# Interleaved weight halves and reversed dense passes in a two-block transformer kernel on one core

## The reference

```
h  = rms(x) * g1                # 512 x 1024
z  = h @ w_in                   # RWKV, retention, window attention, and 3 gates of 1024
x += (sum of sigmoid(gate_b) * (mixer_b(z) @ w_o_b)) @ w_out
x += (silu(rms(x)*g2 @ w_gate) * (rms(x)*g2 @ w_up)) @ w_down
```

## Time and profile before

| quantity | us |
|---|---|
| median of 2 runs | 2548.85 (2546.43 to 2551.27) |
| the profiled execution | 2548.05 |
| span of its instructions | 2546.2 |
| PE busy | 2511.3, 99% of the span |
| POOL busy | 1512.5, 59% |
| DVE busy | 1311.4, 52% |

### The profile page before, as it was taken

One profiled execution on the slowest core, in us unless ns is written; L12 is line 12 of the kernel. 1 busy time (PEld: TensorE's weight loads), 2 busy tenths in 40 slices (PEclk: granted clock), 3 DMA queues, 4 the chain that ended last, 5 costly groups with the idle time before them and its releaser, 6 DMA issues.

```text
span 2546.2 us, 47105 instructions
## 1 busy us (share of the span) xinstructions
PE 2511.3 (99%) x16344; PEld 2012.3 (79%) x16344; DVE 1311.4 (52%) x1979; ACT 691.6 (27%) x1290; POOL 1512.5 (59%) x963
## 2 busy tenths in 40 slices
PE   8989999999999999999999999999999999999999
PEld 6868888887877778888888888867678888888887
DVE  7867555465566657663322224566647663322224
ACT  4452000024135446521100002134446531100002
POOL 5666666656646455556666666645454556666665
PEclk9999999999999999999999999999999999999999
DMA  4213222223211122223222223211122223222223
GB/s 167 71 43 119 91 99 99 91 86 117 92 51 52 44 97 69 72 87 103 93 97 99 96 93 122 91 47 50 51 97 67 75 87 103 91 99 95 95 99 99
DMA packets 72442, 222.55 MB, mean 87 GB/s; under 512 B 9312, under 2 KB 12256, under 8 KB 72288
## 3 DMA queue, kind: packets, MB, share of 16 engines
q1 hardware_dynamic: 71856, 220.36, 26.3%
q10 hardware_dynamic: 432, 0.14, 0.0%
HBM read 218.37 MB, written 2.10 MB: 87 GB/s over the span
## 4 chain that ended last, share of the span: by engine, by line
PE 92%; DVE 4%; DVEq 1%; issue 1%; DMA 1%; POOL 1%; ACT 0%; ACTq 0%; POOLq 0%; SPq 0%
PE acc L550 80%; PE bank L550 10%; DMA raw<-in_w_pg 1%; PE bank L1214 0%; POOL w_lo L376 0%; DVE sumsq L1252 0%; DVE y_lo L1252 0%; DVE bank L1252 0%; DVE xg_lo L1345 0%; POOL w_hi L369 0%; DVE bank L1611 0%; DMA vec<-in_vec 0%; DVE att L1464 0%; DVEq L1412 0%; DVEq L1709 0%
## 5 line engine op out<-in xcount | busy, mean ns | idle before, releaser
L376 POOL TENSOR_TENSOR w_lo<-raw,w_hi 128x1024 fp32r<-128x1024 f32 (+3 forms) x438 | 961.8, 2196 | 301.3 <-PE acc L550 242.1
L369 POOL TENSOR_SCALAR w_hi<-raw 128x1024 fp32r<-128x1024 f32 (+3 forms) x438 | 438.2, 1000 | 584.1 <-PE acc L550 503.1
L550 PE MATMUL acc<-xg_hi,w_hi 128*128 128x512 f32 x2208 | 581.8, 397 | 6.7 <-DVE xg_lo L1345 2.9
L550 PE MATMUL acc<-xg_lo,w_hi 128*128 128x512 f32 x2208 | 568.8, 393 | 0.0
L550 PE MATMUL acc<-xg_hi,w_lo 128*128 128x512 f32 x2208 | 562.7, 393 | 0.2 <-POOL w_lo L376 0.2
L550 PEld LDWEIGHTS acc<-xg_hi,w_hi 128*128 128x128 f32 x2208 | 408.6, 188 | 107.1 <-issue 20.9
L550 PEld LDWEIGHTS acc<-xg_hi,w_lo 128*128 128x128 f32 x2208 | 411.3, 188 | 88.4 <-issue 1.5
L550 PEld LDWEIGHTS acc<-xg_lo,w_hi 128*128 128x128 f32 x2208 | 411.2, 188 | 87.4 <-issue 1.5
L2131 ACT ACTIVATE ffn_act<-ffn_t 128x512 f32<-128x512 f32 x100 | 63.2, 632 | 742.6 <-DVEq L1312 600.7
L1252 DVE TENSOR_TENSOR x<-x,acc 128x512 f32<-128x512 f32 x104 | 71.3, 686 | 311.1 <-PE acc L550 310.6
L1252 DVE TENSOR_TENSOR bank<-acc,rstd 128x512 f32<-128x512 f32 x72 | 50.3, 699 | 263.4 <-PE acc L550 263.3
(11 more groups left out here) (351 smaller groups left out, 2708.4 us busy)
## 6 DMA issues: line engine op xcount, KB each, us to landing
raw<-in_w_up SPq DMA_DIRECT2D x132, 512.0 KB, 3.2
raw<-in_w_down SPq DMA_DIRECT2D x48, 512.0 KB, 3.2
raw<-in_w_gate SPq DMA_DIRECT2D x48, 512.0 KB, 3.2
raw<-in_w_ret SPq DMA_DIRECT2D x32, 512.0 KB, 3.3
raw<-in_w_rw SPq DMA_DIRECT2D x28, 512.0 KB, 3.2
raw<-in_w_o SPq DMA_DIRECT2D x48, 256.0 KB, 2.7
raw<-in_w_in SPq DMA_DIRECT2D x18, 512.0 KB, 3.2
raw<-in_w_down SPq DMA_DIRECT2D x24, 384.0 KB, 3.0
```

The costliest lines, as they stand in the source:

```text
L369: nc.gpsimd.tensor_scalar(w_hi[:, s, 0:n], raw[:, s, 0:n], 1.0, 0.0, ALU.mult, ALU.add).then_inc(w_half[s], 1)
L376: nc.gpsimd.tensor_tensor(w_lo[:, s, 0:n], raw[:, s, 0:n], bits(w_hi[:, s, 0:n]), ALU.subtract).then_inc(w_split[s], 1)
L550: return nc.tensor.matmul(o, a, b, start=first, stop=last, skip_group_check=shared)
```

## The change

It does three things.

1. `w_hi` and `w_lo` become one tensor `halves` of shape (2, 1024, 2): a column's high half and its low half are neighbours, and `w_hi`, `w_lo` are views of it with a step of 8 bytes between columns. The tile that PE loads is spread over 1024 bytes instead of 512. POOL's two instructions write, and one of them reads, with that step. Every tile begins at remainder 128 modulo 512 (high) or 132 (low).
2. A new helper `dense` reverses the token order of a pass: the activations are read from the last token to the first, and PSUM is written in that order. Every dense pass goes through it. The other matmuls stay as they are.
3. The split activations get start remainders of their own: xg 256, y (first block) 192, z_rw, z_rt and with them y1, y2, hid 320, emb 256. The distance from the weight tiles, which was 0, becomes 128 bytes for xg and emb, 64 for y of the first block, 192 for y1, y2 and hid. The assertion that all are equal goes.

```diff
-LINE, START = 512, 128
+LINE = 512
...
-        xg_hi, _ = place("xg_hi", (DC, T), F32R, line=START)
-        xg_lo, _ = place("xg_lo", (DC, T), F32R, line=START)
+        xg_hi, _ = place("xg_hi", (DC, T), F32R, line=256)
+        xg_lo, _ = place("xg_lo", (DC, T), F32R, line=256)
...
-        raw, _ = place("raw", (2, DC * P), line=START)
-        w_hi, _ = place("w_hi", (2, DC * P), F32R)
-        w_lo, _ = place("w_lo", (2, DC * P), F32R)
+        raw, _ = place("raw", (2, DC * P), line=128)
+        halves, _ = place("halves", (2, DC * P, 2), F32R)
+        w_hi, w_lo = (halves[:, :, :, h] for h in range(2))
...
-        y_hi, _ = place("y_hi", (DC, T), F32R, line=START)
-        y_lo, _ = place("y_lo", (DC, T), F32R, line=START)
+        y_hi, _ = place("y_hi", (DC, T), F32R, line=192)
+        y_lo, _ = place("y_lo", (DC, T), F32R, line=192)
...
-        z_rw, rw_at = place("z_rw", (14, T), line=START)
+        z_rw, rw_at = place("z_rw", (14, T), line=320)
...
-        emb_at = base + 24 * 1024 + (START - base) % LINE
+        emb_at = base + 24 * 1024 + (256 - base) % LINE
...
+            def dense(o, a, b, first, last, shared=False):
+
+                return mm(o[:, ::-1], a, b[:, ::-1], first, last, shared)
...
-                        last = mm(o[:], columns_of(w, s, k), v[:, c, :], v is hi and m == 0 and k == 0, m == 1 and k == n - 1)
+                        last = dense(o[:], columns_of(w, s, k), v[:, c, :], v is hi and m == 0 and k == 0, m == 1 and k == n - 1)
...
```

More of the change, by code:

```diff
@@ L180, in build @@
         emb, _ = place("emb", (2, T), F32, offset=emb_at + C4)
-        assert {a % LINE for a in (rw_at, rt_at, emb_at)} == {START} and emb_at + 3 * C4 // 2 <= rt_at and base + 4 * sum(int(np.prod(shape)) for _, shape in FIRST) <= emb_at
+        assert emb_at + 3 * C4 // 2 <= rt_at and base + 4 * sum(int(np.prod(shape)) for _, shape in FIRST) <= emb_at
         rw = {}
@@ L592, in late @@
                     for k, c in enumerate(chunks[:-1]):
-                        mm(acc[s][:], columns_of(w_lo, s, k), a[0][:, c, :], False, False)
+                        dense(acc[s][:], columns_of(w_lo, s, k), a[0][:, c, :], False, False)
                     if stat is not None:
@@ L606, in late @@
                     pe.sem_inc(pe_turn, 1)
-                    mm(acc[s][:], columns_of(w_hi, s, k), a[0][:, c, :], i == 0, False)
-                    last_hi = mm(acc[s][:], columns_of(w_hi, s, k), a[1][:, c, :], False, False)
-                    last = mm(acc[s][:], columns_of(w_lo, s, k), a[0][:, c, :], False, i == n - 1)
+                    dense(acc[s][:], columns_of(w_hi, s, k), a[0][:, c, :], i == 0, False)
+                    last_hi = dense(acc[s][:], columns_of(w_hi, s, k), a[1][:, c, :], False, False)
+                    last = dense(acc[s][:], columns_of(w_lo, s, k), a[0][:, c, :], False, i == n - 1)
                 last_hi.then_inc(hi_done[s], 1)
@@ L620, in three @@
             def three(s, a, k, first, last):
-                mm(acc[s][:], columns_of(w_hi, s, k), a[0][:, k, :], first, False)
-                hi_pass = mm(acc[s][:], columns_of(w_hi, s, k), a[1][:, k, :], False, False)
-                return hi_pass, mm(acc[s][:], columns_of(w_lo, s, k), a[0][:, k, :], False, last)
+                dense(acc[s][:], columns_of(w_hi, s, k), a[0][:, k, :], first, False)
+                hi_pass = dense(acc[s][:], columns_of(w_hi, s, k), a[1][:, k, :], False, False)
+                return hi_pass, dense(acc[s][:], columns_of(w_lo, s, k), a[0][:, k, :], False, last)
             def hid_slots(I, n, count, ahead=0):
@@ L817, in _ @@
                 w = columns_of(w_hi, 0, c)
-                mm(acc[0][:], w, xg_hi[:, c, :], c == 0, False)
-                last = mm(acc[0][:], w, xg_lo[:, c, :], False, False)
+                dense(acc[0][:], w, xg_hi[:, c, :], c == 0, False)
+                last = dense(acc[0][:], w, xg_lo[:, c, :], False, False)
             last.then_inc(hi_done[0], 1)
@@ L822, in _ @@
             for c in full:
-                last = mm(acc[0][:], columns_of(w_lo, 0, c), xg_hi[:, c, :], False, c == DC - 1)
+                last = dense(acc[0][:], columns_of(w_lo, 0, c), xg_hi[:, c, :], False, c == DC - 1)
                 if c < DC - 1:
@@ L833, in one @@
                 def one(s, w, v, c, first=False, last=False):
-                    return mm(acc[s][:], columns_of(w, s, c), v[:, c, :], first, last, True)
+                    return dense(acc[s][:], columns_of(w, s, c), v[:, c, :], first, last, True)
                 def started(s):
@@ L888, in part @@
                         w, v, c = (w_hi, w_hi, w_lo)[k // DC], (xg_hi, xg_lo, xg_hi)[k // DC], k % DC
-                        last = mm(acc[s][:], columns_of(w, s, c), v[:, c, :], k == 0, k == 3 * DC - 1, True)
+                        last = dense(acc[s][:], columns_of(w, s, c), v[:, c, :], k == 0, k == 3 * DC - 1, True)
                         if k == 2 * DC - 1:
```

10 lines of the change are left out of this document (5 added, 5 removed).

## The result

The changed kernel takes 2603.31 us (median of 2 runs, 2602.49 to 2604.13) against 2548.85: the ratio is 1.0219, with an interval of 1.0201 to 1.0238. It is slower by 54 us, where 96 us less were forecast. Its profiled execution took 2604.13 us with a span of 2602.3.

The account below looks back on a forecast made before the run. The prediction took PE's dense passes to bound the kernel. From 2548.05 us, minus 98 (pace), minus 5 (first passes), plus 8 (less hidden) gave 2453; likeliest case 2440 to 2475, wide range 2440 to 2600.

Parts of the forecast that it names:

- What bounds the kernel: Opening step: PE busy 99% at full clock; dense passes set the time, each 226.7 ns, 13.3 beyond its columns.
- Part 1: Pace of the dense passes: reversed order, 8-byte columns and distances keep weight and activation reads apart, 98 us less.
- the price of 216.3 ns: Assumed length of a dense pass after the change, 213.3 + 3 ns, taken from the float32 overhead.
- The 5 us for first passes: Further gain: some 240 stretches begin out of phase, about 4 passes each 5 ns over the pace.
- The sign named for them: Sign of being right: first passes behind small matmuls run at the same pace as later ones.
- no gain: Rival for the dense passes: the 10.4 ns stay, pace 226.7, time 2535 to 2560; chance 0.20.
- Slower, by a denser weight read: Rival: a tile over 1024 bytes doubles the 10.4 ns, a pass 237 ns, 2646 or 2673 us; chance 0.17.
- partial: Rival: only xg passes gain, or all gain half; 2483 or about 2500, between 2475 and 2525; chance 0.16.
- the term of minus 98 us: Main term of the sum: 9408 dense passes, each 10.4 ns shorter.
- Part 2: POOL's split instructions with 8-byte step: no change taken; covered by PE until they grow by a factor of 1.5.
- Part 3: What becomes late: shorter passes hide less DVE and ACT work in RWKV pairs and at stage starts; 8 us back.
- its 8 us: Loss added to the sum: half of 8 us gained in RWKV pairs, and as much again at stage starts.

Follow-up runs that it names:

- e5: Kernel before with 19 series of 48 dense-like passes appended on PE, one thing varied per series: 226.7 ns a pass as before, 233.3 with activations backwards.
- e6: Kernel before with 35 other series of 48 passes appended, varying repeated tokens, shifts, tile width and pass length: 215.8 ns with 8 tokens repeated, 241.9 with 16.
- e1: Kernel before with only the token order of the dense passes reversed, halves contiguous, all start remainders 128: 2599.07 us, ratio 1.020.
- e2: Kernel before with only the weight halves interleaved (8-byte columns), passes forward, all starts at 128: 2601.69 us, ratio 1.0211.
- e3: Kernel before with only the activations' start remainders changed, halves contiguous, passes forward: 2592.71 us, ratio 1.0177.
- e4: Changed kernel without its new distances: 8-byte columns and reversed order, all start remainders 128: 2614.28 us, ratio 1.0263.
- e8: Kernel before with the weight halves moved 16 bytes later (low halves 16 + 256), passes forward: 2584.97 us, ratio 1.0145.
- e9: Kernel before with dense passes taking tokens in runs of 32 bytes at every 128 bytes, PSUM written alike: 2567.11 us, ratio 1.0074.

## Why the prediction was wrong

**What bounds the kernel** was right: PE at 99% with a full clock, and the passes' pace sets the time. So was the arithmetic of the lever: a shift of 6.67 ns a pass is 58 us.

**Part 1 failed** at the step "some 10.4 ns appear only where the moving operand streams at full rate ... two read streams that meet in the same part of SBUF could", and with it at the price of 216.3 ns. The first half holds: float32 passes have 429.2 = 426.7 + 2.5 ns, repeated tokens 215.8 = 213.3 + 2.5, and at 1.2 GHz passes of the plain kind have 426.7 and no surcharge at all (e5). The second half doesn't. Loads of 32 columns or of one repeated column leave 231.8 and 231.7 (e5), and a backward read keeps its 20 ns beside a load of 32 columns (e6). The surcharge doesn't shrink with what the load reads; a quarter of the columns to load makes the pass longer by 5 ns. What a pass without any load would take, no run shows. That the pace depends on phase was read rightly; the 230 ns of first passes were passes ahead of a good state, 226.7, into which distance 0 always settled. Nothing in the trace of before showed a pass of 512 columns without a full load beside it, so the share of the load was an inference; one short series could have measured it.

From this the three edits fall one by one. Reversal: it costs 6.67 ns by itself (e1; in the series 233.3 with PSUM forward, 226.7 with only PSUM backwards). 8-byte columns: the same (e2), with no gain from the matched pace; all six distances give 233.3. Distances: they lose the good state (e3: 232.5 and 233.3), and in the changed kernel the two other edits have lost it already; there they only keep the passes out of the 236.7 ns of e4.

The 5 us for first passes didn't come either. The sign named for them did, first and later passes at the same pace (233.5 and 233.3 ns by starts), but because the later ones became as slow as the first.

The Trainium skill's rule of two independent read ports (TensorE: Matmul & The Clock Gate, Part 2) was put under "no gain". The runs agree with it in that a smaller load doesn't shorten the pass; that the place of the load still moves the pace by 2 to 7 ns is more than it says. The 215.7 ns that the Trainium skill gives there for 512 columns were met here only with at most 8 tokens repeated, or with each of 256 taken twice (215.8).

**The rivals.** "Slower, by a denser weight read" had the sign and, with 2646, was 43 us too high; its mechanism fell, since e1 reads as dense as before and costs the same. What its sentence on PSUM left open is measured in e5: PSUM written in reversed order has 226.7 ns, no cost. "No gain" and "partial" fell. The range ended at 2600 and the result is 2603.3: the prediction weighed a price for PSUM written backwards and none for activations read backwards, though the trace before has no row of such a read. In the sum, the term of minus 98 us (10.4 ns a pass) should have been plus 58 (6.67 ns a pass, less the first passes).

**Part 2** was right: POOL's instructions grew by 8% and 1%, far from the 1.5 at which they would have mattered, and PE waited 1.0 us for them (0.7 + 0.3).

**Part 3** was right that nothing becomes late, with 3.4 us against 3.3; its 8 us were for shorter passes, which didn't come.

**What stays open.** Why a forward read has a good state of 13.3 ns and others 18 to 20, why the step lies between 32 and 64 bytes, whether the period is 256 bytes for every distance, what sets the cycle into which a stretch falls, and whether the surcharge would be there without any load. The runs show these figures and not the structure behind them.

## What to carry to other kernels

Before a stall is put down to two streams that meet, run the pass with one of them made tiny: 48 passes with a 32-column tile would have taken away the reason for this change, and 48 read backwards would have priced it. Change order, step and distance one at a time: three edits with one common condition each cost the whole, and their sum says nothing. And a pace from a bare series is one of the states of that pass; only the kernel, with its interruptions, tells which it gets (220.0 in a series; in the kernel 220.0 and 230.7, in the mean 228.8). Look at the pace stretch by stretch: the mean of 234 in e4 hid two paces, 233.3 and 236.7.

## What the runs showed of the hardware

- A float32r pass of 512 columns at 2.4 GHz costs 213.3 + 2.5 ns when its activations cover at most 32 bytes or each is taken twice; with 64 bytes repeated it takes 241.9, with 128 bytes 236.6, and from 256 bytes on 226.7 (e6). At the granted 1.2 GHz it takes 426.7, which is its columns alone (e5).
- Activations read backwards cost 20 ns a pass over the columns, forwards 13.3 at distance 0; PSUM written backwards costs nothing (e5).
- The distance between the weight tile's and the activations' start counts and not their addresses: 226.7 at 0 and 256 bytes, 228.9 at 64 and 320, 232.2 to 233.5 at most others. A full 128-column load at distance 0 makes the pass 5 ns shorter than a 32-column load does (e5, e6).
- Paces are repeating cycles of intervals, and a stretch keeps its cycle for hundreds of passes. The same pass, order and distance can fall into different ones within one execution: 226.7 and 233.3 in e8, 220.0 and 230.7 in e9, 233.3 and 236.7 in e4. At distance 0, forwards, with contiguous columns, all 18 long stretches had 226.7.
- In clocks at 2.4 GHz the paces 220.0, 226.7 and 233.3 are 512 + 16, + 32 and + 48, and 236.7 is 512 + 56. That is worked out from these runs; no run shows why.
- POOL writing with a step of 8 bytes: +8% for the high part, +1% for the low part; weight loads with that step: 193 to 197 ns instead of 188.
